# Both decay matrices of a state-space mixer built by the vector engine, with one wide exponential each

## The reference, cut to what matters

```python
acum = jnp.cumsum(a_, axis=1)
seg = acum[:, :, None] - acum[:, None, :]
decay = jnp.exp(jnp.where(lower, seg, -jnp.inf))
cb = jnp.einsum('bign,bjgn->bijg', c_, b_)
y_intra = jnp.einsum('bijg,bijgr,bjgr,bjgrp->bigrp', cb, decay, dt_, x_)
```

## Time and profile before

| | before |
|---|---|
| median of three runs | 2229.24 us (2227.0 to 2232.21) |
| the profiled execution | 2228.91 us, span 2227.1 us, mean granted clock 0.971 |
| TensorE busy | 2112.6 us (95%) |
| DVE busy | 1487.7 us (67%) |
| ACT busy | 1208.3 us (54%) |
| GpSimd busy | 62.7 us (3%), 16 masks |

### The profile page before, as it was taken

One profiled execution on the slowest core, in us unless ns is written; L12 is line 12 of the kernel. 1 busy time (PEld: TensorE's weight loads), 2 busy tenths in 40 slices (PEclk: granted clock), 3 DMA queues, 4 the chain that ended last, 5 costly groups with the idle time before them and its releaser, 6 DMA issues.

```text
span 2227.1 us, 26875 instructions
## 1 busy us (share of the span) xinstructions
PE 2112.6 (95%) x11268; PEld 1706.9 (77%) x11268; DVE 1487.7 (67%) x1421; ACT 1208.3 (54%) x1256; POOL 62.7 (3%) x20
## 2 busy tenths in 40 slices
PE   6899999989899999989878999999999999999997
PEld 4678888767677777868567888888888888888885
DVE  3578888753333232235646888898888988888885
ACT  4566665632322222224646767676767666676763
POOL 0111111100000000000000000000000000000000
PEclk9999999989899999999988999999999999999998
DMA  7233454522244544322215999899998989999891
GB/s 310 90 140 133 173 199 157 191 76 76 90 175 152 180 160 157 113 99 97 114 60 215 365 339 353 340 360 355 343 355 343 353 338 351 343 368 347 344 353 54
DMA packets 71776, 510.08 MB, mean 229 GB/s; under 512 B 7968, under 2 KB 8352, under 8 KB 10976
## 3 DMA queue, kind: packets, MB, share of 16 engines
q1 hardware_dynamic: 71568, 508.15, 60.3%
q10 hardware_dynamic: 80, 0.13, 0.0%
HBM read 504.97 MB, written 3.28 MB: 228 GB/s over the span
## 4 chain that ended last, share of the span: by engine, by line
PE 82%; DVE 10%; ACT 4%; issue 2%; DMA 1%; SPq 0%; POOL 0%; POOLq 0%; DVEq 0%; ACTq 0%
PE ps L1086 14%; PE ps L1084 14%; PE ps L1085 14%; PE ps L659 10%; PE ps L661 10%; PE ps L660 10%; PE ps L778 1%; DVE area L1804 1%; PE ps L1068 1%; PE ps L1115 1%; PE ps L671 1%; DVE d_lo L1675 1%; DVE area L1855 1%; DVE area L1832 1%; PE ps L1145 1%
## 5 line engine op out<-in xcount | busy, mean ns | idle before, releaser
L2137 DVE TENSOR_TENSOR w_lo<-w_raw,w_hi 128x2048 fp32r<-128x2048 f32 x336 | 748.5, 2287 | 59.0 <-ACT w_hi L1551 59.0
L1551 ACT ACTIVATE w_hi<-w_raw 128x2048 fp32r<-128x2048 f32 x336 | 625.3, 1919 | 77.2 <-PE ps L1086 76.0
L1675 DVE TENSOR_TENSOR d_lo<-d_raw,d_hi 128x2048 fp32r<-128x2048 f32 (+1 forms) x76 | 171.9, 2262 | 317.2 <-ACT d_hi L1255 317.2
L1084 PE MATMUL ps<-w_hi,x_hi 128*128 128x512 f32 x896 | 358.5, 400 | 5.1 <-DVE x_lo L2192 5.1
L1086 PE MATMUL ps<-w_hi,x_lo 128*128 128x512 f32 x896 | 356.3, 398 | 0.0
L1085 PE MATMUL ps<-w_lo,x_hi 128*128 128x512 f32 x896 | 351.9, 393 | 0.0
L659 PE MATMUL ps<-h_top,d_hi 128*128 128x512 f32 (+1 forms) x816 | 329.1, 403 | 19.3 <-DVE h_low L1667 9.5
L1255 ACT ACTIVATE d_hi<-d_raw 128x2048 fp32r<-128x2048 f32 (+1 forms) x76 | 143.8, 1892 | 365.6 <-DMA d_raw<-in_dense 228.2
L661 PE MATMUL ps<-h_top,d_lo 128*128 128x512 f32 (+1 forms) x816 | 320.7, 393 | 0.0
L660 PE MATMUL ps<-h_low,d_hi 128*128 128x512 f32 (+1 forms) x816 | 316.9, 388 | 0.0
L659 PEld LDWEIGHTS ps<-h_top,d_hi 128*128 128x128 f32 x816 | 156.7, 192 | 62.3 <-issue 24.5
(11 more groups left out here) (291 smaller groups left out, 2504.5 us busy)
## 6 DMA issues: line engine op xcount, KB each, us to landing
w_raw<-in_experts SPq DMA_DIRECT2D x336, 1024.0 KB, 4.8
d_raw<-in_dense SPq DMA_DIRECT2D x120, 1024.0 KB, 5.2
area<-acum_rows SPq DMA_DIRECT2D x16, 1024.0 KB, 7.3
d_raw<-in_dense SPq DMA_DIRECT2D x4, 768.0 KB, 4.3
xT<-in_xt SPq DMA_DIRECT2D x4, 512.0 KB, 6.9
gate_rows<-area SPq DMA_DIRECT2D x4, 512.0 KB, 6.7
hT<-gate_rows SPq DMA_DIRECT2D x2, 1024.0 KB, 6.1
cst<-in_consts SPq DMA_DIRECT2D x2, 512.0 KB, 12.9
```

The source lines that it names most:

```text
L1084: mm(o, hi, w_hi[u % HIGH][:, a:a + 512], start=first, stop=False)
L1551: A(w_hi[n % HIGH][:], w_raw[n % RAW][:], ACT.Copy).then_inc(S["whi_done"], 1)
L1675: TT(d_lo[u][:, 0:w], d_raw[u][:, 0:w], d_hi[si % D_HIGH][:, 0:w].bitcast(F32), ALU.subtract)\
L2137: TT(w_lo[n % RAW][:], w_raw[n % RAW][:], w_hi[n % HIGH][:].bitcast(F32), ALU.subtract)\
```

## The change

`segments` makes the difference for both directions: first `seg[1]` from `rowb[1]`, then `seg[0]` from `rowb[0]`, each with four adds of 128 x 512 and a count on `seg_op`. GpSimd masks both in place, each after its count. `segments_back` becomes one exponential of 128 x 2048 without a bias. The order of calls on ACT and DVE stays.

```diff
             for g in range(GROUPS):
                 pl.wait_ge(S["rowb_in"], 32 * g + 32)
                 for d in (1, 0):
-                    if d == 0:
-                        pl.wait_ge(S["seg_op"], g + 1)
+                    pl.wait_ge(S["seg_op"], 2 * g + 2 - d)
                     v = seg[d].rearrange("p h (c i) -> p (h c) i", c=NCH)
-                    pl.affine_select(out=v, in_=rowb[d].rearrange("p h (c i) -> p (h c) i", c=NCH) if d else v,
+                    pl.affine_select(out=v, in_=v,
...
             def segments_back(g):
-                if not g:
-                    act.wait_ge(S["nb_op"], 2)
                 act.wait_ge(S["seg_mask"], 2 * g + 1)
-                for h in range(HPG):
-                    for ch in range(NCH):
-                        v = seg[1][:, h, ch * P:ch * P + P]
-                        j = 32 + 4 * g + h
-                        last = A(v, v, ACT.Exp, bias=nb[:, ch, j:j + 1])
-                last.then_inc(S["e_done"], 1)
+                A(seg[1], seg[1], ACT.Exp).then_inc(S["e_done"], 1)
...
             def segments(g):
                 dv.wait_ge(S["rowb_in"], 32 * g + 32)
-                o = seg[0].rearrange("p h (c i) -> p h c i", c=NCH)
-                i0 = rowb[0].rearrange("p h (c i) -> p h c i", c=NCH)
-                for ch in range(NCH):
-                    a = per_token(nb, 0, g)[:, ch, :].unsqueeze(2).to_broadcast([P, HPG, P])
-                    last = TT(o[:, :, ch, :], i0[:, :, ch, :], a, ALU.add)
-                last.then_inc(S["seg_op"], 1)
+                for d in (1, 0):
+                    o = seg[d].rearrange("p h (c i) -> p h c i", c=NCH)
+                    i0 = rowb[d].rearrange("p h (c i) -> p h c i", c=NCH)
+                    for ch in range(NCH):
+                        a = per_token(nb, d, g)[:, ch, :].unsqueeze(2).to_broadcast([P, HPG, P])
+                        last = TT(o[:, :, ch, :], i0[:, :, ch, :], a, ALU.add)
+                    last.then_inc(S["seg_op"], 1)
```

## The result

The changed kernel takes 2244.27 us in the median of five runs (2240.89 to 2247.11), against 2231.52 for the kernel before (2227.0 to 2232.41, five runs): a ratio of 1.0063 with a 95% interval of 1.0051 to 1.0074. So it is 0.6% slower, by some 14 us; the two medians alone are 12.75 us apart, a ratio of 1.0057, and the two profiled executions 15.4. The forecast was 2245, slower, with a range from 2236 to 2268.

What follows compares the result with a forecast made beforehand. TensorE's own 47.6 us a cycle and a chain through `token_evac` only 0.2 us longer bind together; group delays of 6.15 + 2.5 + 1.55 + 1.3 + 4.2 = 15.7 us on 2228.91 give 2244.6, said as 2245, range 2236 to 2268.

Steps and rivals of the forecast that it cites:

- a later `token_evac` lengthens the cycle nearly one to one: Group loop: from `token_evac` to `outputs` takes 15.17 us, then the same TensorE work follows, so its delay lengthens the cycle.
- time saved on ACT ahead of the banks is worth nothing: ACT saves 2.88 us a group, but already stood idle 0.82 us until TensorE finished the x projection.
- The floor of 47.58 us: Group loop: TensorE's own busy time in a 47.77 us cycle, below which the cycle can't fall.
- The sum: Delays of `token_evac` over all eight groups, less time given back in groups 2 and 5: 15.7 us in all.
- groups 2 and 5: 2.05 us later less 0.81 given back, as backward masks no longer stretch the convolution: +1.24 us each.
- groups 3, 4 and 6: Forward mask ends late behind adds, backward mask and `dense_low`, so `token_evac` starts 2.05 us later in each.
- group 7: Last group: `dense_low`, `gate_low` and `finish` precede the adds, the mask gets in, `token_evac` starts 4.2 us later.
- TensorE's two waits: Group 3: 1.4 us on `finish` before the product of C and B, and 0.8 us before `outputs`.
- The rule of the Trainium skill: GpSimd and two-SBUF-input DVE instructions exclude each other; a mask gets in after at most one more DVE instruction.
- had ACT load its table after the backward mask: Backward exponential on ACT: the 1.28 us table load stays and comes only after the backward mask is done.
- the first rival: Masks lose every boundary and wait for all adds and `dense_low`: 33 us, 2262, up to 2272; chance 0.25.

Runs made afterwards that it cites:

- both_masks_early: Changed kernel with both masks made at the landing, out of the rows, and all eight adds in place behind them: ratio 1.0011 to the kernel before.
- half_masks: Changed kernel with masks over 1024 of 2048 columns, exponentials scaled by 0.001: 1.82 of the 1.94 us a cycle gone; total 3258 us says nothing.
- back_mask_early: Changed kernel with only the backward mask back at the landing, DVE and ACT work the same: ratio 1.0031 to the kernel before.
- early_exps_first: Changed kernel with both masks at the landing and both exponentials ahead of the emptying of the banks on ACT: ratio 0.9992 to the kernel before.
- best_area32: Masks at the landing, exponentials before emptying the banks, groups 0 and 7 reordered, big area moved by 32 bytes: 2204.39 us, 0.9887 to the kernel before.

## Why the prediction was right, point by point

**What binds.** The prediction said that a later `token_evac` lengthens the cycle nearly one to one and that time saved on ACT ahead of the banks is worth nothing. both_masks_early shows the second (2.9 us less on ACT, cycle 47.75), half_masks and back_mask_early the first. The floor of 47.58 us that it gave the cycle was nearly right for these matmuls (47.50 in early_exps_first), but isn't fixed: with the area moved it was 47.11.

**The sum.** From the first add of group 0 to the last `token_evac` the loop took 364.18 us instead of 349.36, 14.8 us more against 15.7 forecast. By groups, forecast and measured: group 0 +1.3 and +1.26; group 1 +1.55 and +1.46; groups 2 and 5 +1.24 and +1.12 each; groups 3, 4 and 6 +2.05 and +1.94 each; group 7 +4.2 and +4.06. TensorE's two waits were forecast as 1.4 and 0.8 us and measured as 1.1 and 0.75 (the second had been 0.2), and the granted clock stayed at 1.00 behind them. The first adds began 1.05 us sooner in this execution, which belongs to the change by nothing shown. The stretch after the last `token_evac` took 1.4 us more, and about half of that is a cost the forecast left out: behind TensorE's wait of 10.06 us in the last group the granted clock was 0.50, the level of 1.2 GHz, for 12 matmuls (474.5 to 479.7), behind the 5.96 us of before for 8 (460.7 to 464.6), and 24 of them took 7.91 us from the first start to the last instead of 7.25. The rest isn't explained. Loop, start and tail together make the 15.2 us between the two spans. That the total of 2245 was met within 1 us is in part luck: the terms of the loop came out 0.9 us smaller, and the median of the kernel before was 2.3 us above the 2229.24 that the forecast started from.

**The masks.** Forecast 2.3 to 2.5 us for the backward mask with the adds stretched by 1.8, and 3.9 for the forward one: 2.17 to 2.26 and 3.93, adds stretched by 1.8. The convolution was no longer held. The rule of the Trainium skill that I had weighed ("SBUF — State Buffer", section "SBUF: two separate sides": the loser blocks until the holder's instruction is over) gave the right outcome in seven of eight groups; in the last one the mask waited through three more adds, so it is not the whole rule.

**Two steps were wrong, and they cancelled.** I had ACT load its table after the backward mask; in every group it was loaded while ACT waited (252.48 in group 3, mask done at 256.46). In groups 1 to 6 this was worth nothing, since the forward mask ended later than either way (262.28 in group 3). In group 7 the backward mask lost, as the first rival has it, and that rival's price for the group was +5.3 us, with the load behind the mask. With the load made beforehand 1.28 us of it went, which leaves +4.0, and +4.06 was measured, where +4.2 had been forecast for a mask that gets in. So one group's number was met by two errors. Had the mask got in there, the earlier load alone would have changed nothing in the forecast, in which the forward mask, done at 455.15, set the time and not the backward exponential, done at 454.5.

**What stays open.** Why a mask that asks during a run of DVE instructions sometimes gets in at the next boundary and sometimes waits for all of them. Neither the moment within the instruction nor the kind of instruction decides: in back_mask_early one mask asked 0.384 us into an instruction of the convolution and waited, another 0.392 us into one and got in, and during adds the last group's waited where seven alike did not. What the changed kernel would take if all masks lost (the first rival's 2262) was not tried, since nothing that I could set decides it.

## What to carry to other kernels

Ask of work that is moved to an idle engine not how busy that engine is but who must be done before it may start, and whose instructions it can't run beside: here a mask of 2 us, moved behind adds, came 4 us late on the only chain that counted, and the time saved on ACT lay before a wait. The same masks made at the landing of their input, with the column term added behind them, keep the wide exponentials at a cost of 0.1% (1.0011), and are 0.25% faster together with three changes of order. And before a difference of under 1% is put down to an edit, see whether the edit has moved any tile: 32 bytes were worth more here than everything else tried.

## What the runs showed of the hardware that was not expected

The place of a tile in SBUF changes how long matmuls take. Where the big area begins at byte 117760 of each partition (a multiple of 1024, so of 64 too), the experts' matmuls of 128 x 512 shown above took 391 to 397 ns; at 117728, 32 bytes past a multiple of 64, 393 to 400 ns; at 117792, also 32 bytes past one, 395 to 398. With no instruction changed the kernel took 0.9902 (0.9887 to 0.9918) and 0.9985 (0.9976 to 0.9994) of the time before, and TensorE was busy for 2089.8 and 2108.9 us instead of 2112.6. The mixer's cycle fell as well, from 47.50 to 47.11 us with the changes of order in (best_area32).

That the area's begin should be a multiple of 64 fits both moves, but so does a multiple of anything up to 1024, and it isn't simply that each matmul's own operands should begin there. The 128 x 128 operand of these matmuls lies ahead of the small tile and did not move. `w_hi` moved with the area. `w_lo` takes turns among eleven places, six of them ahead of the small tile: the matmuls of L1085 that read one of those six have no operand that moved, and yet the next matmul began 228.5, 226.5 and 233.1 ns after them (means over the whole stage, breaks over 300 ns left out, at 117728, 117760 and 117792). The other five places are at a multiple of 64 exactly when the area's begin is not, and there it was 231.8, 230.2 and 230.8 ns. The matmuls on either side of these read `w_hi`, which did move. What it is about the places that counts stays open.
